# Second projections taken from the unscaled residual, with the norm applied as each tile is read

## What is computed

```python
    h = rmsnorm(h, final_norm)                      # end of the first block
    ...
    u = rms_norm(h, norm1_g[i])                     # start of the second
    p_rwkv, p_nsa = jnp.split(u @ w_in[i], [N_RWKV_COLS], axis=-1)
    y_rwkv = rwkv7_time_mix(p_rwkv, mu, ...)        # p = p + mu * (p_prev - p), then decay, rate, gate, state
    y_nsa = nsa_attention(p_nsa, ...)               # compressed, selected and window attention
    y = jnp.concatenate([y_rwkv, y_nsa], axis=-1)
    h = h + y @ w_out[i]
    h = h + swiglu(rms_norm(h, norm2_g[i]), w_gate, w_up, w_down)
    return rms_norm(h, norm_f_g)
```

## Time and profile before

| | |
|---|---|
| median of 3 runs | 738.89 us (736.79 to 739.21) |
| the profiled execution | 737.27 us |
| its span in the trace | 735.5 us |
| busy: TensorE, weight load | 714.8 us (97%), 638.7 us (87%) |
| busy: VectorE, ScalarE, GpSimd | 517.3 us (70%), 418.1 us (57%), 15.8 us (2%) |
| chain that ended last | TensorE 86%, VectorE 6%, ScalarE 4%, issue 2%, DMA 2% |

### The profile page before, as it was taken

The page is one execution under the profiler, slowest core; times in us unless marked ns, Lnnn a source line. Parts: engine busy times, 40 slices in busy tenths (PEclk is TensorE's granted clock), DMA queues, the critical chain, the costliest instruction groups (busy, mean ns, idle before and its releaser), DMA issues.

```text
span 735.5 us, 15927 instructions
## 1 busy us (share of the span) xinstructions
PE 714.8 (97%) x6362; PEld 638.7 (87%) x6362; DVE 517.3 (70%) x938; ACT 418.1 (57%) x738; POOL 15.8 (2%) x23
## 2 busy tenths in 40 slices
PE   6999999999999999998999999999999999999996
PEld 5877878988888889997888898898988888889995
DVE  4574557778999994448667975574679999985345
ACT  5554555665766664337887653442576666664332
POOL 0000000110000000001000000000020000000000
PEclk9999999999999999999999999999999999999999
DMA  6631332446765555551543333311335555555531
GB/s 237 211 139 58 115 115 68 164 162 243 262 223 180 206 184 176 185 197 71 176 168 115 117 115 117 118 61 60 111 121 214 186 180 207 183 176 199 196 115 58
DMA packets 16738, 113.78 MB, mean 155 GB/s; under 512 B 2000, under 2 KB 2128, under 8 KB 3632
## 3 DMA queue, kind: packets, MB, share of 16 engines
q1 hardware_dynamic: 15984, 109.22, 42.0%
q0 software_dynamic: 704, 3.85, 1.6%
HBM read 112.01 MB, written 1.05 MB: 154 GB/s over the span
## 4 chain that ended last, share of the span: by engine, by line
PE 86%; DVE 6%; ACT 4%; issue 2%; DMA 2%; SPq 0%; DVEq 0%; ACTq 0%
PE ps L602 22%; PE ps L577 12%; PE ps L604 11%; PE ps L579 11%; PE ps L578 11%; PE ps L959 6%; ACT w_hi L1441 1%; DVE w_lo L1924 1%; DMA ring<-in_weights 1%; PE ps L1109 1%; PE ps L1026 1%; DVE acts L2126 1%; DMA vec<-in_vecs 1%; PE ps L1038 1%; DVE res L2118 1%
## 5 line engine op out<-in xcount | busy, mean ns | idle before, releaser
L1924 DVE TENSOR_TENSOR w_lo<-ring,w_hi 128x1024 fp32r<-128x1024 f32 x193 | 235.6, 1222 | 98.2 <-ACT w_hi L1441 96.6
L1441 ACT ACTIVATE w_hi<-ring 128x1024 fp32r<-128x1024 f32 x193 | 203.4, 1055 | 109.6 <-PE ps L579 96.1
L602 PE MATMUL ps<-acts,w_hi 128*128 128x512 f32 x704 | 246.5, 393 | 0.7 <-ACT act_in L1594 0.7
L604 PE MATMUL ps<-acts,w_lo 128*128 128x256 f32 x704 | 197.4, 280 | 0.0
L602 PEld LDWEIGHTS ps<-acts,w_hi 128*128 128x128 f32 x704 | 132.2, 188 | 31.3 <-DVE acts L2126 1.9
L577 PE MATMUL ps<-acts,w_hi 128*128 128x256 f32 (+1 forms) x456 | 136.8, 300 | 1.5 <-DVE w_lo L1924 0.8
L604 PEld LDWEIGHTS ps<-acts,w_lo 128*128 128x128 f32 x704 | 132.3, 188 | 0.1
L579 PE MATMUL ps<-acts,w_lo 128*128 128x256 f32 (+1 forms) x456 | 129.4, 284 | 0.0
L578 PE MATMUL ps<-acts,w_hi 128*128 128x256 f32 (+1 forms) x456 | 129.1, 283 | 0.0
L577 PE MATMUL ps<-hid_hi,w_hi 128*128 (+1 forms) x352 | 99.6, 283 | 0.0
L579 PE MATMUL ps<-hid_hi,w_lo 128*128 (+1 forms) x352 | 99.6, 283 | 0.0
(11 more groups left out here) (372 smaller groups left out, 900.0 us busy)
## 6 DMA issues: line engine op xcount, KB each, us to landing
ring<-in_weights SPq DMA_DIRECT2D x101, 1024.0 KB, 4.8
res<-in_xT SPq DMA_DIRECT2D x2, 544.0 KB, 4.0
ring<-in_weights SPq DMA_DIRECT2D x2, 512.0 KB, 5.2
cst<-in_consts POOLq DMA_DIRECT2D x1, 1024.0 KB, 5.1
out_features<-yT SPq DMA_DIRECT2D x4, 256.0 KB, 2.2
cst<-in_consts POOLq DMA_DIRECT2D x1, 945.5 KB, 4.9
vec<-in_vecs POOLq DMA_DIRECT2D x1, 677.0 KB, 4.2
cst<-in_consts POOLq DMA_DIRECT2D x1, 656.0 KB, 10.3
```

The costliest lines, as they stand in the source:

```text
L602: pe.matmul(ps[:, bank, :].rearrange("p (x t) -> p x t", x=2), w_hi[:, slot, k, :], acts[:, :, at, 0:SEQ], start=(k == 0), stop=(k == KT - ...
L604: return pe.matmul(ps[:, bank, 0:SEQ], w_lo[:, slot, k, :], act_hi[:, at, 0:SEQ], start=False, stop=(k == KT - 1), skip_group_check=True)
L1441: act.activation(w_hi[:, t % SLOTS].rearrange("p k c -> p (k c)"), ring[:, b % RING, half].rearrange("p k c -> p (k c)"), ACT.Copy)\
L1924: dve.tensor_tensor(w_lo[:, t % SLOTS].rearrange("p k c -> p (k c)"), ring[:, b % RING, half].rearrange("p k c -> p (k c)"), w_hi[:, t % S ...
```

## The change

The products of the second projections no longer wait for the norm. Tile `k` of the residual is multiplied by the joint gain of both norms (`gain34`), rounded by ScalarE and rested by VectorE as soon as `add_down` has written it; the factor per token is applied when VectorE reads a projection tile out of its bank (`take_second`), which it now does for all 25 tiles. ScalarE no longer copies tiles: for shifted ones it reads VectorE's result. The gain goes into the narrow tile's weights (`branch_w`).

The rest follows from that. The gained squares are added in three pairs by VectorE and summed in five products ahead of the last round of tiles 0 and 1. The plain squares are added by GpSimd and summed by one product before tile 7, and the residual for later is scaled behind the projections. The first two reads and shifts stand ahead of all splitting in the rounds, `decay_and_rate` comes after tile 3, and the scan for the decay one round later. In VectorE's even rounds, reading, scaling and maxima stand ahead of the split and the shift. The banks are dealt out anew (tile 0 in bank 1, tile 1 in bank 2).

```diff
 def bank2(t):
-    return 6 if t == 2 else t % 2
+    return {0: 1, 1: 2, 2: 6}.get(t, (t + 1) % 2)
...
@@ GpSimd
             signal(pool, pool.memset(blk[:], 0.0), "blk_zeroed")
+            for k in range(1, KT):
+                pool.wait_ge(S("plain_squares"), k + 1)
+                if k > 1:
+                    pool.wait_ge(S("plain_gathered"), k - 1)
+                pool.tensor_tensor(sq_plain[:, 0, :], sq_plain[:, 0, :], sq_plain[:, k, :], ALU.add)\
+                    .then_inc(S("plain_gathered"), 1)
...
@@ TensorE
-            for at, k in enumerate((0, KT - 2, KT - 1)):
...
-            for at, k in enumerate((4, 5, 6, 7, 0)):
...
+            def gained_sums():
+                for at, k in enumerate((0, 2, 4, KT - 2, KT - 1)):
...
+            def plain_sum():
+                pe.wait_ge(S("plain_gathered"), KT - 1)
+                pe.wait_ge(S("values_kept"), 1)
+                pe.matmul(ps[:, 2, 0:SEQ], C("ones"), sq_plain[:, 0, :], start=True, stop=True)\
+                    .then_inc(S("plain_sums"), 1)
...
             for k in range(KT):
+                if k == KT - 1:
+                    gained_sums()
                 pe.wait_ge(S("normed"), normed("norm4", k))
...
             for t in range(2, TILES2):
-                if t == 3:
+                if t == 4:
+                    pe.wait_ge(S("proj2_taken"), 2)
                     decay_and_rate()
...
+                if t == 7:
+                    plain_sum()
...
-                if t > 2 and is_shifted(t - 2):
-                    pe.wait_ge(S("shifted"), shifted_upto(t - 2))
-                elif t > 4:
-                    pe.wait_ge(S("proj2_plain"), plain_upto(t - 2))
+                if t > 4:
+                    pe.wait_ge(S("proj2_taken"), t - 1)
...
@@ ScalarE
+            for k in range(KT):
+                act.wait_ge(S("down_added"), k + 1)
+                act.activation(act_hi[:, k, 0:SEQ], res[:, k, META:CTX], ACT.Copy, scale=gain34[:, k:k + 1])\
+                    .then_inc(S("act_rounded"), 1)
                 gained_square(k)
+            split_hi(T_IN2 + GL0 + 1)
+            for k in range(KT):
                 plain_square(k)
...
+            def shift_scaled(t):
+                k = shifted_upto(t) - 1
+                act.wait_ge(S("proj2_taken"), t + 1)
...
-                if t + SLOTS < TILES2:
+                if t + SLOTS < TILES2 and t != 0:
                     split_hi(T_IN2 + t + SLOTS)
+                if is_shifted(t) and t != 1:
+                    shift_scaled(t)
                 if t == 0:
+                    shift_scaled(1)
+                    act.preload_act_table_set("sigmoid_and_others")
+                    split_hi(T_IN2 + SLOTS)
                     act.wait_ge(S("shifted"), 1)
...
@@ VectorE
+            for k in range(KT):
+                if k + 1 < KT:
+                    add_down(1, k + 1)
+                rest_residual(k)
+            for k in (1, 3, 5):
+                gather_gained(k)
...
+            def take_second(t):
+                dve.wait_ge(S("proj2_ready"), t + 1)
+                dve.scalar_tensor_tensor(proj2[:, t, :], ps[:, bank2(t), 0:SEQ],
+                                         HD ** -0.5 if Q0 <= t < Q0 + 4 else 1.0, nrm[:, 0, 0:SEQ], ALU.mult,
+                                         ALU.mult).then_inc(S("proj2_taken"), 1)
...
+                if t == 0:
+                    dve.wait_ge(S("norm_root"), nth("norm3"))
+                    take_second(0)
+                    take_second(1)
+                    shift(0)
+                    shift(1)
+                elif t > GL0:
+                    take_second(t)
+                if t % 2 == 0 and 0 <= (t - 8) // 2 < UNITS:
+                    nsa_scaled((t - 8) // 2)
+                if t % 2 == 0 and 0 <= (t - 6) // 2 < UNITS:
+                    nsa_maxima((t - 6) // 2)
                 if t + SLOTS < TILES2:
                     split_lo(T_IN2 + t + SLOTS)
+                if t > 1 and is_shifted(t):
+                    shift(t)
```

More of the change, by code:

```diff
@@ L2240, in _, with rest_residual @@
[L2240 to L2245 removed]
+            def rest_residual(k):
+                dve.wait_ge(S("act_rounded"), rounded("norm4", k))
+                dve.wait_ge(S("down_added"), k + 1)
+                dve.scalar_tensor_tensor(act_lo[:, k, 0:SEQ], res[:, k, META:CTX], gain34[:, k:k + 1],
+                                         act_hi[:, k, 0:SEQ].bitcast(F32), ALU.mult, ALU.subtract)\
+                    .then_inc(S("normed"), 1)
@@ L2296, in nsa_kept, with shift @@
                 ins.then_inc(S("nsa_out_kept"), 1)
+            def take_second(t):
[3 more added lines that the diff above has]
+                                         ALU.mult).then_inc(S("proj2_taken"), 1)
+            def shift(t):
+                k = shifted_upto(t) - 1
+                dve.wait_ge(S("shift_scaled"), k + 1)
+                dve.scalar_tensor_tensor(proj2[:, t, :], proj2[:, t, :], om_mu[:, k:k + 1], shift_buf[:, k % 2, 0:SEQ],
+                                         ALU.mult, ALU.add).then_inc(S("shifted"), 1)
             def key_sums_kept(f):
@@ L2408, in _ @@
             fill_xt(0, 1)
+            residual_scaled(0)
             fill_xi(1, 1)
```

146 lines of the change are left out of this document (53 added, 93 removed).

## The result

| | before | changed |
|---|---|---|
| median, us | 738.40 (736.79 to 740.31) | 741.56 (740.13 to 744.07) |
| profiled execution, us | 737.27, span 735.5 | 740.63, span 738.8 |
| TensorE / VectorE busy, us | 714.8 / 517.3 | 715.2 / 521.4 |
| end of the last projection tile | 440.78 | 444.17 |

The ratio is 1.0041, with an interval of 1.0026 to 1.0056: slower by some 3 us, more than the 0.3% that a measurement can tell. The changed kernel's numbers leave out one execution of 1400.58 us, nearly twice the others and never repeated. The whole difference is there when the projections end (3.4 us in the trace; the last down product starts at 336.30, 336.40 before), so it lies between the last down product and tile 24.

The account below looks back on a forecast made before the run. TensorE was taken to bound the kernel, with VectorE full beside it. Terms of -1.6 + 0.4 - 0.3 + 3.25 gave +1.8 us, set on a mean of 738.0: 739.8 us, range 735.5 to 743.0.

Parts of the forecast that it names:

- Part 1: Handover to the second projections: narrow products 4.2 us earlier, mostly given back in a 3.5 us fold pause; -1.6 us.
- rival 2: At tile 3's fold: the clock falls in TensorE's stall, adding 1.9 us; +3.7 us in all, 741.7 us; chance 0.20.
- Part 2: Work moved on TensorE: plain sum ahead of tile 7 costs +0.4 us, the pause at 378.17 goes for -0.3 us.
- Part 3: VectorE's read of every projection tile: waits at key sums and before later values, +3.25 us, bounds 0 and 5.
- Rival 1: In the projections: VectorE's pauses absorb the reads, so only the handover counts; -1.9 us, 736.1 us; chance 0.28.
- two couplings: In the projections: key squares wait for VectorE's late shift (+0.45 us twice), and ScalarE's shift multiply waits for VectorE's read.
- the second coupling: ScalarE's shift multiply waits for VectorE's read, delaying exponentials and weights; waits of 0.15, 1.1, 1.5 us before tiles 19, 21, 23.

Follow-up runs that it names:

- six more reads: Changed kernel with VectorE reading each of tiles 16 to 21 once more into spare space, of no use to the output: 744.23 us.
- reads undone: Changed kernel without VectorE's reads of tiles 16 to 21, taken straight from the banks as before, their multiplication by the norm left out: 740.06 us.
- filler: Changed kernel with 26 useless TensorE products put ahead of the fold's wait: 741.73 us, and 740.90 us when measured again.
- two shifts first: Changed kernel with VectorE's shifts of tiles 12 and 14 put ahead of the weight split of their round: 740.38 us.
- packs on GpSimd: Changed kernel with ScalarE's narrow copy and exponentials and VectorE's two shifts moved earlier, plus three VectorE packing products given to GpSimd: 741.14 us.

## Why the prediction was right, and where it was not

The sign and the places held, 741.56 lies in the range of 735.5 to 743.0, and parts 2 and 3 came out by their own mechanism. Part 1 did not: the clock fell behind the fold, which the prediction had named as a sign that it was wrong. The likeliest time, 739.8, was 1.8 us too low, and most of that is this fall; the case that came true is rival 2, put at 0.20, whose 741.7 is 0.1 off. The time lies in the range because the range was made wide enough to take in rival 2, not because the working behind 739.8 held. By its own steps:

- **Part 1, the handover: the step that failed.** Narrow products at 344.33 (344.6), pause at the fold 3.42 (3.5), both as worked out. From there I took 2.08 for the fold with four rounds and 1.92 for decay and rate, from rows at the full clock. They took 353.43 - 350.43 = 3.00 and 2.64. The term was -1.6 and measured -0.17. This is rival 2 to the letter, put at +1.9 and measured at 1.4 (-0.17 against -1.6) to 1.55 (14.69 against 13.14). My argument against it, that the longest pause so far was 1.48 and nothing showed a fall in mid-run, only said that nothing had tested it. I had the row that spoke for it: the clock fell some 4 us after TensorE's last product. Here the last product before the pause ended at 347.01 and the clock fell near 351.5, 4.5 us later (2.6 to 4.4 in the four other traces with this fall); that TensorE had begun again at 350.43 did not stop it. A pause of 3.5 beside a fall at 4 deserved more than 0.20. The Trainium skill, "TensorE: Matmul & The Clock Gate", Part 1, states that an idle array drops to 1.2 GHz and needs sustained work to rise again. The trace agrees: 0.50 from 352, and 1.00 again from 355, with TensorE at work without a pause from 350.43.
- **Part 2.** From tile 4's start to tile 12's end the changed kernel took 34.13 and the kernel before 34.02, so +0.11 where +0.4 - 0.3 stood. The pause at the turn at 378 is gone, and the residual's scalings, moved behind the projections, cost nothing that the traces show (from the projections' end to the span's end 294.6 us, 294.7 before). GpSimd's adds ran from 342.5 to 348.6, and beside them the first two shifts took 1.36 us together, where two instructions of that form take 0.88 elsewhere (L2356 at 417.80); TensorE did not wait for them.
- **Part 3.** +3.25 predicted, 53.97 - 50.52 = +3.45 measured. Key sums 0.43 and 0.43 (0.45 each); values before tile 19 none (0.15), before 21 1.19 (1.1), before 23 1.36 (1.5); the turn's 0.41 gone. The pauses come to 3.0 more than before. The other 0.45 is what the stops cost beside the counted pause, 0.23 each at the key sums, which the sum had not counted; so the total agrees with +3.25 as well as it does partly by luck.
- **Rival 1** is out: TensorE did not run through tiles 13 to 24 as before. Its premise, that VectorE absorbs the reads, is refuted from both sides by the six more reads and the reads undone.
- **The sum.** -0.17 + 0.11 + 3.45 = +3.4 in the trace; the medians differ by 3.2. Rival 2's sum was +3.7 and its time 741.7.
- **Part 3's cause** was named as two couplings beside the reads' own time, and the experiments part them. The key sums' waits are order: two shifts moved, both gone. The values' waits are amount of work: reordering ScalarE only handed them to VectorE, so ScalarE's tie to the reads, the second coupling, was where the wait showed and not what it came from.

Not settled: why the filler's saved 1.55 us does not appear in its medians, where in its timed executions the clock falls, and in which of the changed kernel's timed executions the fall is the one at the fold.

## What to carry to other kernels

When a change lets one engine run ahead, look at once for the first thing that it must fetch from a slower one, and put the producer of that thing first in its queue: here one copy of 0.36 us, moved ahead of a table load, decided between 0.4% slower than before and no slower. A long pause of TensorE is to be costed with a fall of the clock beside it: here eight of the nine pauses of 2 us or more between the first product and the last had one, and at the fold it cost 1.5 us more (2.7 once). And where an engine beside the bound is full for tens of microseconds, as VectorE was here, expect each added instruction on it to be paid (0.31 of 0.33 here). Reordering ScalarE or VectorE's own packing moved the wait, GpSimd beside VectorE made it worse, and what removed it was taking reads off VectorE, at the price of a bank held longer.

## What the hardware showed that I had not expected

**The clock can fall after the pause is over,** as above. The moment varies: worked out from slices of 1 us, the fall came 1.1 and 0.2 us after TensorE had resumed in the two traces of the changed kernel, 1.0 after with the two shifts first, 0.1 after with the six reads, and 0.8 before the end of the pause with the reads undone. The clock stayed low for some 3.4 us in the first four, and for 6.8 with the reads undone. That kernel, whose pause of 3.42 ended at 351.71:

```profile
348.00:352.00 4.00, 0.58 (x4) 0.26 (x3) 2.57 (x3) 3.99 (x7) 1.63 (x3) 0.86 0.02 8
```

After pauses of 1.19 to 1.85 no fall was seen; after 2.01 and 2.04 one was, each time; after 3.42, five times in six; the one of 5.29 had its fall as it ended.

**It also fell with no pause at all.** With the two shifts first, and with the packs on GpSimd, a fall stands near 492, in slices in which the profile has TensorE busy throughout, with small products (64x64 and less); no trace of the other kernels has it there. Nor is the kernel before free of it: 5 of its 22 executions taken beside the first experiments have a mean granted clock of 0.995 and times of 738.88 to 739.84 us, above their median of 738.26, though its longest pause is 1.48. The kernel with the two shifts first:

```profile
490.00:491.00 1.00, 1.00 (x28) 0.93 (x24) 0.47 (x1) 0.00 (x0) 0.00 (x0) 1.00 0.63 98
491.00:492.00 1.00, 1.00 (x14) 0.75 (x12) 0.00 (x0) 0.00 (x0) 0.00 (x0) 0.80 0.84 336
492.00:493.00 1.00, 1.00 (x21) 1.00 (x22) 0.91 (x4) 0.00 (x0) 0.00 (x0) 0.50 1.02 434
```

**The start varies.** The first projection's products ran at half rate for up to 4.7 us in some executions, though the granted clock in those stretches is given as 1.00. So the granted clock does not show everything that slows TensorE. The filler's first trace, and the changed kernel's:

```profile
11.44 0.43 PE L580 MATMUL ps<-acts,w_hi 128*128 128x272 f32 x1
11.67 0.43 PE L581 MATMUL ps<-acts,w_lo 128*128 128x272 f32 x1
```

```profile
11.07 0.29 PE L580 MATMUL ps<-acts,w_hi 128*128 128x272 f32 x1
11.20 0.29 PE L581 MATMUL ps<-acts,w_lo 128*128 128x272 f32 x1
```

Starts 0.23 apart in the one, 0.13 in the other; the next stage begins at 16.29 in the one and 13.97 in the other, 2.3 us later, before any edited line has run. (The pause of TensorE ahead of its first product is the same to 0.1 us in both.) This is larger than most of the differences studied here, which is why the lengths inside the traces decide above, and the medians only where they agree with them.
